# Hybrid decoder step on one core: first tile of x rounded by the Vector engine, queries taken out before a late weight chunk, keys turned before a subtraction, first softmax scaled by the Scalar engine

## The chip, the core and the metric

One core of a Trainium2 chip runs the whole program. The metric is the device time of one execution in microseconds, and a version is judged by the median of its runs. TensorE (PE) multiplies matrices, the Vector engine (DVE), the Scalar engine (ACT) and GpSimd (POOL) do elementwise work, and SyncE (SP) issues most of the loads.

## What is computed

The reference is one layer of a decoder for a prompt of 256 tokens and eight sample tokens, 264 columns in all, in fp32. Cut to what the change touches:

```
h = rmsnorm(x, g_mix)
proj = h @ w_in                       # pool channels | q | k | v, 512 columns each
q = rope(proj q); k = rope(proj k)    # 8 heads x 64
logits = q k^T * 64**-0.5, causal     # 256 x 256 per head for the prompt
p = softmax(logits);  attn = p v
x = x + concat(pool_out, attn) @ w_out
x = x + cross_attention(rmsnorm(x), memory)
x = x + relu(rmsnorm(x) @ w_up)**2 @ w_down
y = rmsnorm(x, g_final)
```

## The kernel before

**Products in three parts.** Every fp32 operand is split in a rounded part and a remainder ("hi" and "lo", both fp32r), and a product is hi\*hi + lo\*hi + hi\*lo. The weights stream through in 120 chunks of 256 rows by 512 columns. Per chunk SP loads `raw`, ACT copies it with rounding into `w_hi` (`split_hi`, line 1106 in the rows, since the helper `copy` records every ACT copy), and DVE subtracts into `w_lo` (`split_lo`, L1362). PE then runs 24 matmuls of 264 columns (four banks of 128 output rows, two row tiles, three passes, L1086). The splits run some chunks ahead: a chunk's `w_hi` goes into one of four buffers and waits until PE has used the chunk four before; its raw buffer is reloaded when an earlier chunk's `w_lo` is done.

**Start.** PE warms up with ten small fp32 matmuls (`warm_up`, L998). Then chunks 0 to 2 go row tile by row tile in `open_first_group` (L1010, L1013, L1016): hi weights on hi x, lo weights on hi x, hi weights on lo x, four matmuls each. ACT rounds the weights and x tile by tile; DVE makes both remainders. From chunk 3 on the ordinary loop runs.

**Groups and jobs.** Four chunks of `w_in` make one group: chunks 0 to 3 give the queries (banks 0 to 3), 4 to 7 the keys, 8 to 11 the values, 12 to 15 the pool channels `uext`. Each engine has its own program in one hand-written order. For every chunk it takes out the results of a finished group (`take_out`), does its share of the splits (`split_next`), and runs the jobs that the table in `plan_jobs` puts there. A ("split",) in that table says where among the jobs the split stands. Where a group ends and no such entry is there, `halfway` puts the split between the second and the third tile taken out.

**Jobs named later.** ("stat", "x"), after chunk 4, sums the squares of x on PE (L851, L855) in bank 0, which held the first query tile; ACT takes the root (L1258), DVE the reciprocal (L1556), and `turn_tables` multiplies the cosine and sine tables. ("turn", 0) turns the first pair of query tiles and ("turn", 2) the first pair of key tiles, four DVE instructions each (L1444 to L1448). ("S", 0) to ("S", 3), after chunk 8, are the scores of the first four heads (L829); PE waits in one place for both turns and for four free banks. ("exp", h) is on ACT; ("norm", 0), after chunk 13, inverts the row sums of four heads (L1534) and multiplies the four score tiles (L1539), both on DVE. ("P_T", h) transposes a head's probabilities on PE (L869), and ACT copies them out (`softT`). After chunk 15 come the scores of heads 4 to 7, in banks 3, 0, 1 and 4. Banks 3, 0 and 1 come free by the `softT` copies of heads 0 to 2, and bank 4 when DVE has taken out the first `uext` tile (L1403). ("v_nat", 0) and ("v_nat", 1), after chunks 12 and 13, are transposes of the values (L864) that ACT copies out and stores by a DMA of its own queue. ("m_tile", k) and ("m_lo", k) split the memory; each m_tile also makes a square that POOL adds (L1650).

Of the kernel before, what the change touches and what calls it, by code (L numbers as in the profile page):

```python
# [143 lines left out]


def plan_jobs():

# [17 lines left out]
    put(1, ("sum_x",), ("split",))  # L165
    put(2, ("split",))
    put(4, ("stat", "x"), ("tables",), ("split",), ("turn", 0))
    put(5, ("m_tile", 0))
    put(7, ("turn", 2), ("split",), ("m_tile", 1), ("m_tile", 2))
    put(8, ("m_tile", 3), ("m_lo", 0), ("m_lo", 1), ("m_lo", 2), ("S", 0), ("S", 1), ("S", 2), ("S", 3))  # L170
# [41 lines left out]

SCALED_BY_ACT = ()

# [205 lines left out]
def build(nc, ins, outs):  # L420
    with ExitStack() as ctx:
# [385 lines left out]
        def _(pe):  # L807
# [192 lines left out]
            def open_first_group():  # L1000

                for c in range(PARTED):
                    g, w, n, k, _ = CHUNKS[c]
                    hi, lo = hi_of(c), lo_of(c)
                    banks = banks_of(g)
                    for kk in range(CK):
                        pe.wait_ge(first_hi_ready, k + kk + 1)
                        pe.wait_ge(stream_hi, k + kk + 1)
                        for x, bank in enumerate(banks):
                            pe.matmul(psum[:, bank, 0:T], hi[:, kk, x * P:(x + 1) * P], act_hi[:, k + kk, :], start=k + kk == 0, stop=False)  # L1010
                        pe.wait_ge(first_lo_ready, k + kk + 1)
                        for x, bank in enumerate(banks):
                            pe.matmul(psum[:, bank, 0:T], lo[:, kk, x * P:(x + 1) * P], act_hi[:, k + kk, :], start=False, stop=False)  # L1013
                        pe.wait_ge(stream_lo, k + kk + 1)
                        for x, bank in enumerate(banks):
                            mm = pe.matmul(psum[:, bank, 0:T], hi[:, kk, x * P:(x + 1) * P], act_lo[:, k + kk, :], start=False, stop=False)  # L1016
                    mm.then_inc(w_used, 1)
# [86 lines left out]
        def _(act):  # L1104
# [35 lines left out]
            def take_out(c):  # L1140
# [3 lines left out]
                for x, bank in enumerate(banks_of(g)):  # L1144
                    src = psum[:, bank, 0:T]
                    k = AT * n + x
                    if x == 2 and halfway(c):
                        for s in SPLITS_AT.get(c + 1, ()):
                            split_hi(s)
# [159 lines left out]
            def split_next(c):  # L1309
                for s in SPLITS_AT.get(c + 1, ()):  # L1310
                    split_hi(s)

# [9 lines left out]
            for c in range(PARTED):  # L1322
                for kk in range(CK):
# [4 lines left out]
                    copy(hi_of(c)[:, kk, :], raw_of(c)[:, kk, :]).then_inc(first_hi_ready, 1)  # L1328
                    k = CK * c + kk
                    act.wait_ge(x_landed[k if k < 4 else CK * c], 16)  # L1330
                    copy(act_hi[:, k, :], xT[:, k, :], gains[:, GAIN["x"], k:k + 1]).then_inc(stream_hi, 1)
            round_x(3)
            for s in SPLITS_AT[0]:
                split_hi(s)
            for c in range(NC):
                if c == STAT_X:
                    act.wait_ge(tables_landed, 16)
                if CHUNKS[c][4]:
                    take_out(c)
                if not halfway(c) and ("split",) not in JOBS[c]:  # L1340
                    split_next(c)
# [8 lines left out]
        def _(dve):  # L1350
# [236 lines left out]
            def less_x(k):  # L1587
                dve.wait_ge(stream_hi, k + 1)
                less(act_lo[:, k, :], xT[:, k, :], gains[:, GAIN["x"], k:k + 1], act_hi[:, k, :]).then_inc(stream_lo, 1)

            dve.wait_ge(x_landed[0], 16)
            for c in range(PARTED):
                for kk in range(CK):
                    k = CK * c + kk
                    dve.wait_ge(first_hi_ready, k + 1)
                    V.tensor_tensor(lo_of(c)[:, kk, :], raw_of(c)[:, kk, :], hi_of(c)[:, kk, :].bitcast(F32), ALU.subtract).then_inc(first_lo_ready, 1)
                    less_x(k)
            for k in range(CK * PARTED, KT):
# [148 lines left out]
```

## Time and profile before

| | us |
|---|---|
| median of 3 runs (422.76, 421.59, 422.97) | 422.76 |
| the profiled execution's own time | 422.28 |
| its span in the profile | 420.1 |
| PE busy | 413.4 (98%) |
| DVE busy | 252.9 (60%) |
| ACT busy | 226.8 (54%) |
| granted TensorE clock, whole span | 0.999 |

The span is the stretch between the first and the last record. 2.18 us of the execution's own time lie outside it. A matmul's end is modelled: in a steady row a matmul is shown as 0.28 us long while the next begins 0.12 us after it, so a stall is best read from start to start, not from the idle time that is printed.

### The profile page before, as it was taken

How to read it: one execution, taken by the hardware profiler on the slowest of the kernel's cores; microseconds unless marked ns; L12 is line 12 of the kernel's file. 1: busy time of each engine (PE TensorE's matmuls, PEld its weight loads, DVE VectorE, ACT ScalarE, POOL GpSimd, SP SyncE). 2: the span in 40 equal slices, each digit the busy share in tenths (PEclk: the TensorE clock that was granted, in tenths of full speed). 3: DMA queues.
4: the chain of work that ended last, by engine and by line, in shares of the span. 5: the costliest groups of instructions: out<-in, count | busy, mean ns of one | idle time of the engine just before them, and what ended most of it. 6: DMA issues, size and time to landing. Idle time of an engine off the chain costs nothing.

```text
span 420.1 us, 8422 instructions
## 1 busy us (share of the span) xinstructions
PE 413.4 (98%) x3372; PEld 388.5 (92%) x3372; DVE 252.9 (60%) x398; ACT 226.8 (54%) x392; POOL 31.1 (7%) x41
## 2 busy tenths in 40 slices
PE   9999999999999999999999999999999999999995
PEld 8998989986879998958899999999999999999995
DVE  4899989666255785543269677766766534454302
ACT  6776958825364574423267566556565343453313
POOL 1003017000000120000022000000000000010010
PEclk9999999999999999999999999999999999999999
DMA  8999858974989966989527546545456555655002
GB/s 286 382 396 355 274 193 236 344 274 156 373 313 333 383 232 219 369 330 347 206 100 249 203 149 200 195 171 177 165 199 202 197 174 180 196 159 171 2 2 103
DMA packets 37257, 96.60 MB, mean 230 GB/s; under 512 B 4186, under 2 KB 13274, under 8 KB 37082
## 3 DMA queue, kind: packets, MB, share of 16 engines
q1 hardware_dynamic: 35250, 92.50, 63.2%
q10 hardware_dynamic: 1968, 3.55, 2.5%
q8 instruction: 27, 0.44, 0.4%
q14 instruction: 12, 0.10, 0.1%
HBM read 91.73 MB, written 4.54 MB: 229 GB/s over the span
## 4 chain that ended last, share of the span: by engine, by line
PE 90%; DMA 3%; DVE 3%; SPq 1%; issue 1%; ACT 0%; DVEq 0%
PE psum L1086 75%; PE psum L817 5%; PE psum L1031 2%; PE psum L945 2%; DMA raw<-in_w_in 2%; PE psum L932 2%; DMA pages<-in_page_table 1%; PE psum L829 1%; DVE w_lo L1362 1%; PE psum L869 1%; SPq L763 1%; PE psum L878 1%; PE psum L916 1%; PE psum L938 0%; DVE rstd L1556 0%
## 5 line engine op out<-in xcount | busy, mean ns | idle before, releaser
L1362 DVE TENSOR_TENSOR w_lo<-raw,w_hi 128x1024 fp32r<-128x1024 f32 x67 | 82.9, 1247 | 63.1 <-ACT w_hi L1106 62.9
L1106 ACT ACTIVATE w_hi<-raw 128x1024 fp32r<-128x1024 f32 (+1 forms) x73 | 73.9, 1020 | 60.1 <-PE psum L1086 48.0
L1086 PE MATMUL psum<-mix_hi,w_hi 128*128 128x264 f32 (+1 forms) x288 | 82.9, 288 | 0.0
L1086 PE MATMUL psum<-mix_lo,w_hi 128*128 128x264 f32 (+1 forms) x288 | 81.6, 283 | 0.0
L1086 PE MATMUL psum<-mix_hi,w_lo 128*128 128x264 f32 (+1 forms) x288 | 81.6, 283 | 0.0
L1086 PE MATMUL psum<-act_hi,w_hi 128*128 128x264 f32 x232 | 66.9, 288 | 0.0
L1086 PE MATMUL psum<-act_lo,w_hi 128*128 128x264 f32 x232 | 66.0, 284 | 0.0
L1086 PE MATMUL psum<-act_hi,w_lo 128*128 128x264 f32 x232 | 66.0, 284 | 0.0
L1086 PEld LDWEIGHTS psum<-mix_hi,w_hi 128*128 128x128 f32 x288 | 54.3, 189 | 0.9 <-issue 0.8
L1086 PEld LDWEIGHTS psum<-mix_lo,w_hi 128*128 128x128 f32 x288 | 54.2, 188 | 0.1
L1086 PEld LDWEIGHTS psum<-mix_hi,w_lo 128*128 128x128 f32 x288 | 54.1, 188 | 0.0
L1650 POOL TENSOR_TENSOR ssq<-ssq,sq 128x264 f32<-128x264 f32 (+1 forms) x27 | 22.5, 833 | 331.0 <-ACT sq L1127 329.6
L1086 PE MATMUL psum<-hid_hi,w_hi 128*128 128x264 f32 x160 | 45.5, 284 | 0.0
L1086 PE MATMUL psum<-hid_hi,w_lo 128*128 128x264 f32 x160 | 45.5, 284 | 0.0
L1086 PE MATMUL psum<-hid_lo,w_hi 128*128 128x264 f32 x160 | 45.4, 284 | 0.0
L1086 PEld LDWEIGHTS psum<-act_hi,w_hi 128*128 128x128 f32 x232 | 43.8, 189 | 0.4 <-issue 0.3
L1086 PEld LDWEIGHTS psum<-act_lo,w_hi 128*128 128x128 f32 x232 | 43.7, 188 | 0.0
L1086 PEld LDWEIGHTS psum<-act_hi,w_lo 128*128 128x128 f32 x232 | 43.6, 188 | 0.0
L1086 PEld LDWEIGHTS psum<-hid_lo,w_hi 128*128 128x128 f32 x160 | 30.1, 188 | 0.0
L1086 PEld LDWEIGHTS psum<-hid_hi,w_lo 128*128 128x128 f32 x160 | 30.1, 188 | 0.0
L1086 PEld LDWEIGHTS psum<-hid_hi,w_hi 128*128 128x128 f32 x160 | 30.1, 188 | 0.0
L1362 DVE TENSOR_TENSOR w_lo<-raw_more,w_hi 128x1024 fp32r<-128x1024 f32 x16 | 19.5, 1230 | 15.3 <-ACT w_hi L1106 15.3
(203 smaller groups left out, 811.1 us busy)
## 6 DMA issues: line engine op xcount, KB each, us to landing
raw<-in_w_down SPq DMA_DIRECT2D x20, 512.0 KB, 4.2
raw<-in_w_up SPq DMA_DIRECT2D x18, 512.0 KB, 3.7
raw_more<-in_w_up SPq DMA_DIRECT2D x14, 512.0 KB, 3.8
stage<-in_mem_v SPq DMA_DIRECT2D x12, 512.0 KB, 5.9
raw_more<-in_w_down SPq DMA_DIRECT2D x12, 512.0 KB, 4.4
stage<-in_cache_v SPq DMA_DIRECT2D x16, 256.0 KB, 6.5
keysT<-in_cache_k SPq DMA_DIRECT2D x16, 256.0 KB, 4.8
keysT<-in_mem_k SPq DMA_DIRECT2D x8, 512.0 KB, 6.4
```

The source lines that it names most:

```text
L763: sp.dma_start(raw_of(c)[:, kk, :], ins[w_of[w]][n, k // CK][:, kk, :]).then_inc(done, 16)
L817: return pe.matmul(out, lhsT, rhs, start=start, stop=stop, skip_group_check=True, tile_position=(0, 32 * j))
L829: last = pe.matmul(bank_of(job)[:, out:out + keys], qT[r:r + 32, f, queries:queries + P], kT[r:r + 32, f, 0:keys], start=half == 0, stop=h ...
L869: last = pe.transpose(B[:, x * P:(x + 1) * P], p[:, x * P:(x + 1) * P], ident)
L878: pe.matmul(o[:, 0:SEQ], v_nat[:, 0, h * HD:(h + 1) * HD], pT[:, 0:SEQ], start=True, stop=False, skip_group_check=True)
L932: last = pe.matmul(B[:, qt * MEM:(qt + 1) * MEM], q2T[:, 2 * h + d, qt * P:(qt + 1) * P], mkT[:, 2 * h + d, :], start=d == 0, stop=d == 1)
L945: last = pe.matmul(B[:, d * SEQ:(d + 1) * SEQ], mv[:, c, h * MHD + d * P:h * MHD + (d + 1) * P], pT[:, c * SEQ:(c + 1) * SEQ], start=c == ...
L1031: mm = pe.matmul(psum[:, bank, 0:T], a, b, start=False, stop=end_ and m == 2)
L1086: mm = pe.matmul(out, a, b, start=first and m == 0, stop=end_ and m == 2)
L1106: return nc.scalar.activation(out, in_, ACT.Copy, scale=scale)
L1362: V.tensor_tensor(lo_of(c), raw_of(c), hi_of(c).bitcast(F32), ALU.subtract).then_inc(w_lo_ready, 1)
L1650: nc.gpsimd.tensor_tensor(ssq[:, m % 2, 0:n], ssq[:, m % 2, 0:n], sq[:, k % SQ_SLOTS, 0:n], ALU.add).then_inc(sq_added, 1)
```

## The change

Four things are done.

1. DVE rounds the first tile of x (ACT skips it) and makes its remainder at once. PE's second pass on that tile is now hi weights on lo x, and lo weights come third. ACT waits for DVE's rounding before it rounds the second tile.
2. At chunk 3, where the queries are finished, ACT and DVE no longer split chunk 6 before it and chunk 7 halfway; all four query tiles are taken out first, and chunks 6 and 7 are split behind them.
3. ("turn", 2) moves from chunk 7 to chunk 6, ahead of the split of chunk 10.
4. `SCALED_BY_ACT` holds 0: the products of ("norm", 0) become eight ACT copies with a scale, two for each of the heads 0 to 3. DVE only inverts the sums. Heads 4 to 7 stay with DVE.

The core of the diff:

```
+QUERIES = last_chunk("in", 1)
...
     put(1, ("sum_x",), ("split",))
-    put(2, ("split",))
...
-    put(7, ("turn", 2), ("split",), ("m_tile", 1), ("m_tile", 2))
+    put(6, ("turn", 2), ("split",))
+    put(7, ("split",), ("m_tile", 1), ("m_tile", 2))
...
-SCALED_BY_ACT = ()
+SCALED_BY_ACT = (0,)
...
-                    if x == 2 and halfway(c):
+                    if x == 2 and halfway(c) and c != QUERIES:
...
             def split_next(c):
-                for s in SPLITS_AT.get(c + 1, ()):
-                    split_hi(s)
+
+                for at in {QUERIES - 1: (), QUERIES: (QUERIES, QUERIES + 1)}.get(c, (c + 1,)):
+                    for s in SPLITS_AT.get(at, ()):
+                        split_hi(s)
...
                     k = CK * c + kk
+                    if k == 0:
+                        continue
                     act.wait_ge(x_landed[k if k < 4 else CK * c], 16)
+                    if k == 1:
+                        act.wait_ge(stream_hi, 1)
...
             dve.wait_ge(x_landed[0], 16)
+            V.tensor_scalar(act_hi[:, 0, :], xT[:, 0, :], gains[:, GAIN["x"], 0:1], None, ALU.mult).then_inc(stream_hi, 1)
+            less_x(0)
```

The places on ACT and DVE, as the two programs have them (line number, operation, output from inputs, shape; a buffer is named by its tile). **ACT around the end of the queries (chunk 3), before:** the split of chunk 6 stands first, that of chunk 7 in the middle.

```order
L1209 ACTIVATE keysT<-x_and_gains 128x1056 x2
L1106 ACTIVATE w_hi<-more_keysT 128x1024
L1106 ACTIVATE w_hi<-raw 128x1024
L1106 ACTIVATE qT<-psum 128x264 x2
L1106 ACTIVATE w_hi<-raw 128x1024
L1106 ACTIVATE qT<-psum 128x264 x2
L1258 ACTIVATE std<-psum,const 128x266
```

After, in the same place:

```order
L1115 ACTIVATE qT<-psum 128x264 x4
L1115 ACTIVATE w_hi<-raw 128x1024 x2
L1267 ACTIVATE std<-psum,const 128x266
L1115 ACTIVATE w_hi<-raw 128x1024
L1115 ACTIVATE w_hi<-more_keysT 128x1024
```

The four copies of the queries moved ahead of both splits. The copies of chunk 5, as before, stand ahead of them.

**DVE from the query turn to the first scores, before:** the first four rows turn the queries, the second four the keys, with the subtractions of chunks 9 and 10 between them.

```order
L1444 SCALAR_TENSOR_TENSOR crossed<-qT,turned 128x264
L1445 SCALAR_TENSOR_TENSOR crossed<-qT,turned 128x264
L1446 SCALAR_TENSOR_TENSOR qT<-qT,turned 128x528
L1448 TENSOR_TENSOR qT<-qT,crossed 128x528
L1362 TENSOR_TENSOR w_lo<-more_keysT,w_hi 128x1024 x2
L1444 SCALAR_TENSOR_TENSOR crossed<-kT,turned 128x264
L1445 SCALAR_TENSOR_TENSOR crossed<-kT,turned 128x264
L1446 SCALAR_TENSOR_TENSOR kT<-kT,turned 128x528
L1448 TENSOR_TENSOR kT<-kT,crossed 128x528
L1362 TENSOR_TENSOR w_lo<-more_keysT,w_hi 128x1024
```

After:

```order
L1461 SCALAR_TENSOR_TENSOR qT<-qT,turned 128x528
L1463 TENSOR_TENSOR qT<-qT,crossed 128x528
L1377 TENSOR_TENSOR w_lo<-more_keysT,w_hi 128x1024
L1459 SCALAR_TENSOR_TENSOR crossed<-kT,turned 128x264
L1460 SCALAR_TENSOR_TENSOR crossed<-kT,turned 128x264
L1461 SCALAR_TENSOR_TENSOR kT<-kT,turned 128x528
L1463 TENSOR_TENSOR kT<-kT,crossed 128x528
L1377 TENSOR_TENSOR w_lo<-more_keysT,w_hi 128x1024 x2
```

One subtraction (chunk 10) moved from ahead of the keys' turn to behind it.

**ACT after chunk 13, before:** the second value tile, its store, the splits of chunks 17 and 18, a memory tile, and the copies of the transposed heads.

```order
L1106 ACTIVATE v_nat<-psum,rstd 128x512
L1268 DMA out_v_prompt<-v_nat 128x512
L1106 ACTIVATE w_hi<-raw 128x1024 x2
L1127 ACTIVATE sq<-stage 128x256
L1106 ACTIVATE mix_hi<-stage,x_and_gains 128x256
L1106 ACTIVATE softT<-psum 128x384 x3
```

After:

```order
L1277 DMA out_v_prompt<-v_nat 128x512
L1115 ACTIVATE soft<-soft,stats 128x128
L1115 ACTIVATE soft<-soft,stats 128x256
L1115 ACTIVATE soft<-soft,stats 128x128
L1115 ACTIVATE soft<-soft,stats 128x256
L1115 ACTIVATE soft<-soft,stats 128x128
L1115 ACTIVATE soft<-soft,stats 128x256
L1115 ACTIVATE soft<-soft,stats 128x128
L1115 ACTIVATE soft<-soft,stats 128x256
L1115 ACTIVATE w_hi<-raw 128x1024 x2
L1136 ACTIVATE sq<-stage 128x256
L1115 ACTIVATE mix_hi<-stage,x_and_gains 128x256
```

Eight scalings came in ahead of the splits of chunks 17 and 18 and of the copies of the transposed heads. On DVE the two products of L1539 are gone from behind the reciprocal (L1534), and the subtraction of chunk 17 follows it.

## Rows read from the trace of the kernel before

**Rows 1.** The page: span, then busy time, share and instructions of each engine.

```profile
span 420.1 us, 8422 instructions
PE 413.4 (98%) x3372; PEld 388.5 (92%) x3372; DVE 252.9 (60%) x398; ACT 226.8 (54%) x392; POOL 31.1 (7%) x41
```

**Rows 2.** Waits of PE over the span: who for whom, us in total, times, longest.

```profile
PE psum L829 <- DVE kT L1448: 0.6, 1, 0.6
PE psum L851 <- issue: 0.4, 1, 0.4
```

**Rows 3.** Timeline of the start (start us, length us, engine, line, operation).

```profile
5.21 0.42 PE L998 MATMUL psum<-std 128*128 128x128 f32 x1
5.50 0.97 PE L1010 MATMUL psum<-act_hi,w_hi 128*128 128x264 f32 x4
10.03 0.52 ACT L1106 ACTIVATE act_hi<-x_and_gains 128x264 fp32r<-128x264 f32 x1 [0.68 <-DMA x_and_gains<-in_x]
13.28 2.36 DVE L1362 TENSOR_TENSOR w_lo<-more_keysT,w_hi 128x1024 fp32r<-128x1024 f32 x2 [0.27 <-ACT w_hi L1106]
14.56 0.39 PE L1086 MATMUL psum<-act_hi,w_hi 128*128 128x264 f32 x1
```

**Rows 4.** Timeline of ACT and PE around the queries and the sum of x's squares.

```profile
19.65 1.06 ACT L1106 ACTIVATE w_hi<-raw 128x1024 fp32r<-128x1024 f32 x1 [2.40 <-DMA raw<-in_w_in]
20.61 0.65 ACT L1106 ACTIVATE qT<-psum 128x264 f32<-128x264 f32 x2
20.37 0.29 PE L1086 MATMUL psum<-act_hi,w_lo 128*128 128x264 f32 x1
21.08 0.68 PE L851 MATMUL psum<-ssq,const 128*128 128x264 f32 x2 [0.43 <-issue]
```

**Rows 5.** Landing times of the loads issued between 12.5 and 13 us (7.4 and 8.2).

```profile
DMA to landing us min/median/max: 7.4/7.8/8.2
```

**Rows 6.** Timeline of DVE and PE from chunk 7's subtraction to the first scores.

```profile
22.24 1.23 DVE L1362 TENSOR_TENSOR w_lo<-raw,w_hi 128x1024 fp32r<-128x1024 f32 x1 [0.28 <-ACT w_hi L1106]
28.73 0.71 DVE L1448 TENSOR_TENSOR qT<-qT,crossed 128x528 f32<-128x528 f32 x1
29.47 2.36 DVE L1362 TENSOR_TENSOR w_lo<-more_keysT,w_hi 128x1024 fp32r<-128x1024 f32 x2
31.75 0.43 DVE L1444 SCALAR_TENSOR_TENSOR crossed<-kT,turned 128x264 f32<-128x264 f32 x1
33.29 1.14 DVE L1448 TENSOR_TENSOR kT<-kT,crossed 128x528 f32<-128x528 f32 x1
33.60 0.29 PE L1086 MATMUL psum<-act_hi,w_lo 128*128 128x264 f32 x1
34.48 0.73 PE L829 MATMUL psum<-kT,qT 32*128 32x128 f32 x16 [0.60 <-DVE kT L1448]
```

**Rows 7.** Timeline of ACT from the first exponential to the transposed heads.

```profile
42.34 0.40 ACT L1230 ACTIVATE soft<-soft,stats 128x128 f32<-128x128 f32 x1
51.78 0.69 ACT L1106 ACTIVATE v_nat<-psum,rstd 128x512 f32<-128x512 f32 x1 [0.91 <-PE psum L864]
52.94 1.06 ACT L1106 ACTIVATE w_hi<-raw 128x1024 fp32r<-128x1024 f32 x1 [0.47 <-ACT v_nat L1106]
56.04 0.49 ACT L1106 ACTIVATE mix_hi<-stage,x_and_gains 128x256 fp32r<-128x256 f32 x1
56.44 1.23 ACT L1106 ACTIVATE softT<-psum 128x384 f32<-128x384 f32 x3
```

**Rows 8.** Timeline of POOL, DVE and PE before the second scores.

```profile
56.21 1.48 POOL L1650 TENSOR_TENSOR ssq<-ssq,sq 128x256 f32<-128x256 f32 x1 [14.77 <-ACT sq L1127]
57.00 0.97 DVE L1366 SCALAR_TENSOR_TENSOR mix_lo<-stage,x_and_gains,mix_hi 128x256 fp32r<-128x256 f32 x1
58.29 0.42 DVE L1403 TENSOR_TENSOR uext<-psum,rstd 128x264 f32<-128x264 f32 x1
58.86 0.39 PE L829 MATMUL psum<-kT,qT 32*128 32x128 f32 x4
```

More of the change, by code:

```diff
@@ L1010, in open_first_group @@
                             pe.matmul(psum[:, bank, 0:T], hi[:, kk, x * P:(x + 1) * P], act_hi[:, k + kk, :], start=k + kk == 0, stop=False)
+                        if k + kk == 0:
+                            pe.wait_ge(stream_lo, 1)
+                            for x, bank in enumerate(banks):
+                                pe.matmul(psum[:, bank, 0:T], hi[:, kk, x * P:(x + 1) * P], act_lo[:, 0, :], start=False, stop=False)
                         pe.wait_ge(first_lo_ready, k + kk + 1)
                         for x, bank in enumerate(banks):
[L1013 to L1016, printed above, removed]
+                            mm = pe.matmul(psum[:, bank, 0:T], lo[:, kk, x * P:(x + 1) * P], act_hi[:, k + kk, :], start=False, stop=False)
+                        if k + kk > 0:
+                            pe.wait_ge(stream_lo, k + kk + 1)
+                            for x, bank in enumerate(banks):
+                                mm = pe.matmul(psum[:, bank, 0:T], hi[:, kk, x * P:(x + 1) * P], act_lo[:, k + kk, :], start=False, stop=False)
                     mm.then_inc(w_used, 1)
@@ L1339, in _ @@
                     take_out(c)
-                if not halfway(c) and ("split",) not in JOBS[c]:
+                if (not halfway(c) or c == QUERIES) and ("split",) not in JOBS[c]:
                     split_next(c)
@@ L1596, in _ @@
                     V.tensor_tensor(lo_of(c)[:, kk, :], raw_of(c)[:, kk, :], hi_of(c)[:, kk, :].bitcast(F32), ALU.subtract).then_inc(first_lo_ready, 1)
-                    less_x(k)
+                    if k > 0:
+                        less_x(k)
             for k in range(CK * PARTED, KT):
```

## The prediction

> **What bounds the kernel now.** The page first: PE is busy for 413.4 us of the 420.1 [rows 1], so no other engine can set the time, and the time can only change by what PE waits. The list of PE's waits has, apart from the warm-up's start, two entries [rows 2]: 0.6 us at the first scores, which wait for the turned keys, and 0.4 us at the sum of x's squares, which is put down to no one. By the list PE never waits again behind the first scores. So the whole of what can be won lies in the first 35 us, and whatever is won there is PE's only if nothing that had been just in time becomes late. The timelines of the other engines are then read for that: who finishes how shortly before PE needs it.
>
> Matmul ends are modelled, so I take stalls from start to start. In a steady row a matmul starts 0.12 us after the last one. At the sum of squares the step is 21.08 - 20.37 = 0.71 us [rows 4], so PE loses 0.59 us. At the first scores it is 34.48 - 33.60 = 0.88 us [rows 6], so it loses 0.76 us. Together 1.35 us, 0.32% of the time.
>
> **First tile of x by DVE.** PE's first real matmul starts at 5.50, but the last warm-up pass only starts at 5.21 [rows 3], and PE works in order. The ten warm-up matmuls are twenty passes in the 4.4 us up to there, 0.21 us each, so PE isn't free before about 5.42: what an earlier first tile can bring is 0.08 us at once. A little more could come from the order of passes: the first four matmuls take 0.97 us. But it does not get far. Chunk 3 needs its `w_lo`, and that is the first of the two subtractions from 13.28, which ends at about 14.5 (2.36 us less one of 1.15 is 1.21); PE starts chunk 3 at 14.56 [rows 3]. It is just in time already. Its subtraction is set by ACT, which runs without a gap from 10.03 on, and at 10.03 ACT had waited 0.68 us for the fifth tile of x to land [rows 3]. Nothing of the change touches that load, which is issued before. So what PE wins at the start it waits at chunk 3. I count 0.0 us, bounds -0.1 and 0.0 (a loss is excluded as long as DVE has the tile by then, and its two extra-early instructions stand in time in which it was idle).
>
> **Queries first.** The sum of squares uses bank 0, and bank 0 is free when ACT has copied the first query tile. Before, that copy starts at 20.61, behind the rounding of chunk 6, which waited 2.40 us for its load and began at 19.65 [rows 4]. That is PE's 0.59 us. In the changed order ACT has nothing to do from 17.25 on (19.65 less the 2.40 it waited), takes the queries out as they come (chunk 3 ends at about 17.6) and is done by 18.5, in the time it waited. The load of chunk 6 decides its rounding as before, at 19.65. Chunk 7's rounding no longer has two query copies ahead of it, but its load was issued at 12.7 and took 8.2 us [rows 5], so it starts at 20.87 and not at 20.61, where 21.15 was (20.61 plus two copies). PE gets the sum of squares 0.59 us earlier: **-0.59 us**, and the rest is late by nothing: DVE's subtraction of chunk 7 goes from 22.24 [rows 6] to 21.96 and all that stands behind it on DVE comes 0.28 us earlier. The root on ACT now starts at about 21.85, the end of chunk 7's rounding, and is done before DVE wants it at 23.1.
>
> **Keys before the subtraction.** DVE works without a gap from 22.24 to the keys' turn. The turn starts at 31.75, and the two subtractions ahead of it take 2.28 us, 1.14 each [rows 6]. With one of them behind it and DVE 0.28 us ahead, the turn starts at 31.75 - 1.14 - 0.28 = 30.33. The two key tiles that it needs are there by then: chunk 8 ends at 33.72, chunks 7 and 8 are 24 matmuls of 0.122 us each, 2.93 us a chunk, so the first half of chunk 7 is done at 29.33, less 0.59, plus a copy of 0.4: 29.1. Its first three instructions take 33.29 - 31.75 = 1.54 us; the last took 1.14 us, 0.43 us more than the same one on the queries (0.71) [rows 6], which I take for POOL's doing (below). So the turn ends between 30.33 + 1.54 + 0.71 = 32.58 and 33.01. PE, 0.59 us ahead, gets to the scores at 33.60 - 0.59 + 0.12 = 33.13. Either end is in time, so the whole wait goes: **-0.76 us**. The subtraction of chunk 10, now behind the turn, ends by 34.6, and PE wants it at 37.6 (33.13, 1.53 for the scores and a chunk of 2.93). No DMA moves with it, and no load of weights waits for that one subtraction: its raw buffer isn't used again soon. From 33.13 on PE would be 1.35 us ahead of the kernel before.
>
> **Scaling on ACT.** DVE is rid of two products, which is no gain by itself, since it is not DVE's work that is late there before. ACT gets eight copies. The nearest rows for their price: a copy with a scale of 256 columns lasts 0.49 us and the next instruction starts 0.40 us after it (56.04 to 56.44) [rows 7]; an exponential of one of the very tiles, 128 columns, lasts 0.40 us [rows 7], so a step of 0.31. Four heads by 0.31 + 0.40 are 2.84 us. They stand ahead of the roundings of chunks 17 and 18 on ACT. PE needs those chunks only at 66 us, so this looks hidden. But DVE's order is: subtraction of 17, subtraction of 18, two remainders of the memory, and then the first `uext` tile, and PE's second set of scores waits for that tile's bank. Before, that tile starts at 58.29, is done at 58.71, and the scores start at 58.86 [rows 8]: 0.15 us apart, the tightest place of the stage.
>
> Follow it in the changed kernel. The chain begins with the second value tile on ACT, which waits for PE (51.78 [rows 7]), and PE is 1.35 us ahead: 50.43. ACT's own work up to there has room: the exponentials start at 42.34 [rows 7] behind a table load that came when PE's chunk 9 allowed it, and can start by about 41.2, when DVE has the maxima. From the value tile to the next work on ACT are 52.94 - 51.78 = 1.16 us (the copy and the DMA that it issues) [rows 7]: 51.59. The eight scalings: 54.43. Chunk 17's rounding takes a step of 0.96 us, so chunk 18's begins at 55.39 and is done at 56.45. DVE subtracts chunk 17 from 55.51 and chunk 18 from 56.66, 1.15 us each: 57.81. In the kernel before the remainders began at 57.00 and the `uext` tile at 58.29, 1.29 us later [rows 8]. So it starts at 59.10, is done at 59.52, and the scores start at about 59.57, where they were at 58.86. PE, which would have been 1.35 us ahead, waits about 2.06 us: **+2.06 us**. The copies of the transposed heads, also behind the scalings, end at 57.05 + 1.23 = 58.3 and are not last.
>
> The first remainder took 0.97 us (57.00), while POOL was adding a square, from 56.21 to 57.69 [rows 8]; two remainders undisturbed would be some 0.8 us. If POOL's addition falls elsewhere, 0.5 us of the 1.29 go, and the scores start at 59.07. I keep the 0.5, since the square comes at the same place of ACT's order, in chunk 18's subtraction, as before. The transposes of the heads 0 to 3 themselves are not late: the heads are ready at 52.3, 53.0, 53.7 and 54.4, and PE, 1.35 us ahead, wants them from 53.2 in steps of 0.33.
>
> A rule of the Trainium skill speaks against this edit: "ScalarE: Activation LUTs", Rules for kernel authors, gives multiplications to VectorE and not to ScalarE. By the section What ACT_TABLE_LOAD costs on the same page, a copy whose scale is a pointer takes 0.186 + 0.000833 per column in microseconds after overlap, estimated 2.77 us for the eight; the rows' 2.84 agree, and by the page's price the scores would start 0.07 us earlier. The rule compares the engines' speed; what decides here is the place in ACT's order.
>
> **The sum.** -0.59 - 0.76 + 2.06 = +0.71 us, by starts of the second scores 59.57 - 58.86. Behind them PE had no wait, and the stages are led by PE, so it stays: the execution of 422.28 us with its span of 420.1 becomes 423.0 with a span of 420.8. The median of the three runs, 422.76, is 0.48 us above that execution, and a run 1.2 us below it is among the three; I stay with the sum on the profiled time.
>
> **Rivals.** (a) The chain through the scalings is shorter: no POOL addition in the remainders (-0.5), and up to 0.6 us elsewhere, cheaper copies above all. The scores start at 58.5 to 58.9 and the net is -0.4 to 0.0: about 422.0. For it: POOL's addition only has to miss two short instructions. Against it: in the trace it was asked for during chunk 18's subtraction, too, and ran on over the remainder. (b) The scaling costs nothing: the scores don't wait for it, because the `uext` tile or the bank is free otherwise. Then the full 1.35 us are won: 420.9, faster by 0.32%. Against it stands the 0.15 us of slack and the order of DVE. (c) Slower: ACT's own chain ahead of the value tile does not come forward with PE. Its exponentials wait for the maxima, and DVE is only 0.28 us ahead. If the second value tile is copied at 51.5 and not at 50.43, everything behind is 1.07 us later: scores at 60.64, net +1.8, 424.1. It decides from a value tile later than 51.0 on (net over +1.27). For it: from 42.34 on ACT works nearly without a gap up to the value tile; against: its wait of 0.91 us there [rows 7], and exponentials that should begin 1.1 us earlier. (d) The change does not do what it says at the first two places: the load of chunk 7, at 8.2 us of landing, or the turn beside POOL comes later still, and PE is 0.9 us ahead, not 1.35. Since the second scores hang on PE's lead by way of the value tile, net is then about +1.2: 423.4.
>
> **Chances.** Forecast together with (d), -0.2 to +1.27 us: 0.53. (a), -0.2 to -1.27: 0.20. (b): 0.09. (c): 0.18. A measurement of this kernel can tell 0.3%, 1.27 us, from no change. So faster 0.09, same 0.73, slower 0.18. The likeliest time is 423.0. The range leaves out (b) below and the upper part of (c): 421.2 to 424.3.
>
> **What would show it.** In the profile of the changed kernel: PE's step to the sum of squares is 0.1 to 0.2 us and not 0.71; the scores start at about 33.1; chunk 3 starts at 14.5 to 14.6 although the first matmuls start a little earlier; eight ACT copies of 0.3 to 0.4 us stand from about 51.6 to 54.4; and PE has a new wait of 1.5 to 2.1 us at L829 near 57.6, for DVE's `uext`. If that wait is missing or under 1 us, the forecast is wrong and the time is below 422. If the second value tile's copy lies after 51.0, (c) is right. If the keys' turn ends after 33.2, (d).

## The result and the profile after

| | before | after |
|---|---|---|
| median, us | 422.88 (421.25 to 425.12, 20 runs) | 424.60 (422.62 to 425.69, 20 runs) |
| profiled execution's own time, us | 422.28 | 424.76 |
| its span, us | 420.1 | 422.6 |
| its granted clock | 0.999 | 0.996 |

The ratio is 1.0032, with an interval of 1.0019 to 1.0045: the changed kernel is slower by about 1.35 us (0.8 to 1.9). The two medians in the table stand further apart, 1.72 us; the ratio has an interval and is used from here on. The forecast was +0.71 us on the 422.28 of the profiled execution, with a range of 421.2 to 424.3. On that base the ratio gives 423.6 us, inside the range; the plain median of 424.60 lies 0.3 us above its upper end. The loss is about twice the forecast, and it lies just over the 0.3% that were taken as the border of "no change". The difference has to be looked for.

The page of the changed kernel, answering to [rows 1]:

```profile
span 422.6 us, 8428 instructions
PE 415.0 (98%) x3372; PEld 389.0 (92%) x3372; DVE 250.9 (59%) x397; ACT 229.5 (54%) x399; POOL 31.1 (7%) x41
```

PE has as many instructions as before and is "busy" 1.6 us longer. The list of its waits, answering to [rows 2] (who for whom, total, times, longest; the second is the warm-up's start):

```profile
PE psum L832 <- DVE uext L1418: 1.9, 1, 1.9
PE psum L1001 <- POOL std L1672: 1.0, 1, 1.0
```

Both waits of [rows 2] are gone, and one of 1.9 us has come. The timeline of PE, DVE and ACT from the start to the first scores, answering to [rows 3], [rows 4] and [rows 6]:

```profile
5.28 1.04 PE L1013 MATMUL psum<-act_hi,w_hi 128*128 128x264 f32 x4
14.69 0.39 PE L1095 MATMUL psum<-act_hi,w_hi 128*128 128x264 f32 x1
17.28 1.21 ACT L1115 ACTIVATE qT<-psum 128x264 f32<-128x264 f32 x4
19.62 1.06 ACT L1115 ACTIVATE w_hi<-raw 128x1024 fp32r<-128x1024 f32 x1 [1.13 <-DMA raw<-in_w_in]
20.50 0.28 PE L1095 MATMUL psum<-act_hi,w_lo 128*128 128x264 f32 x1
20.62 0.61 PE L854 MATMUL psum<-ssq,const 128*128 128x264 f32 x2
30.38 0.43 DVE L1459 SCALAR_TENSOR_TENSOR crossed<-kT,turned 128x264 f32<-128x264 f32 x1
31.93 0.71 DVE L1463 TENSOR_TENSOR kT<-kT,crossed 128x528 f32<-128x528 f32 x1
33.06 0.29 PE L1095 MATMUL psum<-act_hi,w_lo 128*128 128x264 f32 x1
33.27 0.94 PE L832 MATMUL psum<-kT,qT 32*128 32x128 f32 x20
```

The four query copies stand ahead of chunk 6's rounding, and PE's step to the sum of squares is 20.62 - 20.50 = 0.12 us. The keys' turn begins at 30.38, and the first scores follow the last matmul in 0.21 us: they begin at 33.27, where they began at 34.48. PE's lead is thus 1.21 us in this execution (chunk 3 had begun 0.13 us later than before, at 14.69).

The same for the stretch of the second scores, answering to [rows 7] and [rows 8]:

```profile
50.56 0.69 ACT L1115 ACTIVATE v_nat<-psum,rstd 128x512 f32<-128x512 f32 x1 [0.71 <-PE psum L867]
51.67 2.88 ACT L1115 ACTIVATE soft<-soft,stats 128x128 f32<-128x128 f32 x8 [0.42 <-ACT v_nat L1115]
54.45 1.99 ACT L1115 ACTIVATE w_hi<-raw 128x1024 fp32r<-128x1024 f32 x2
55.53 2.36 DVE L1377 TENSOR_TENSOR w_lo<-raw,w_hi 128x1024 fp32r<-128x1024 f32 x2 [4.48 <-ACT w_hi L1115]
57.81 1.34 DVE L1381 SCALAR_TENSOR_TENSOR mix_lo<-stage,x_and_gains,mix_hi 128x256 fp32r<-128x256 f32 x2
59.08 0.76 DVE L1418 TENSOR_TENSOR uext<-psum,rstd 128x264 f32<-128x264 f32 x2
57.29 0.49 PE L872 MATMUL psum<-const,soft 128*128 128x128 f32 x3
59.64 2.11 PE L832 MATMUL psum<-kT,qT 32*128 32x128 f32 x32 [1.86 <-DVE uext L1418]
61.68 3.06 PE L820 MATMUL psum<-keysT,qblock 128*32 128x257 f32 x32
64.68 0.65 PE L881 MATMUL psum<-softT,v_nat 128*64 128x256 f32 x4
```

DVE stands idle for 4.48 us until ACT, behind its eight scalings, has rounded chunk 17; then it works through its order, and PE gets the bank of the first `uext` tile at 59.64. That is 0.78 us after the 58.86 of [rows 8]. But the two groups of matmuls that follow are also longer. In the kernel before, the scores from 58.86 on were followed by (PE's timeline):

```profile
60.38 1.95 PE L817 MATMUL psum<-keysT,qblock 128*32 128x257 f32 x32
62.26 0.65 PE L878 MATMUL psum<-softT,v_nat 128*64 128x256 f32 x4
```

From the start of the scores to the start of the work behind both groups it was 62.26 - 58.86 = 3.40 us before and is 64.68 - 59.64 = 5.04 us after: 1.64 us more for the same 64 matmuls. The reason stands in the column of the granted clock (a row has the stretch and its length, then busy time and instructions of PE, PEld, DVE, ACT and POOL, then the clock, the share of DMA and GB/s):

```profile
core 0: us, PE busy (x) PEld busy (x) DVE busy (x) ACT busy (x) POOL busy (x), PEclk, DMA share, GB/s
58.00:59.00 1.00, 0.00 (x0) 0.00 (x0) 1.00 (x2) 1.00 (x2) 0.47 (x1) 1.00 0.87 283
60.00:61.00 1.00, 1.00 (x27) 1.00 (x24) 1.00 (x2) 0.00 (x0) 0.00 (x0) 0.79 0.04 16
61.00:62.00 1.00, 1.00 (x12) 0.23 (x11) 1.00 (x4) 0.00 (x0) 0.00 (x0) 0.50 0.06 16
63.00:64.00 1.00, 1.00 (x16) 0.54 (x12) 1.00 (x9) 1.00 (x4) 0.72 (x1) 0.51 0.34 47
64.00:65.00 1.00, 1.00 (x20) 0.40 (x14) 0.97 (x4) 0.56 (x3) 0.94 (x2) 1.00 0.00 0
```

PE does nothing in the whole microsecond from 58. About 0.9 us after it has begun again, at 60.6, its clock falls to 0.50, the lower of its two levels (1.2 of 2.4 GHz), and stays there until about 64. In the kernel before the column reads 1.00 in every one of these microseconds. So in this execution the loss of 2.5 us in span is 0.78 us of position and 1.64 us of clock (together 2.42). The clock of the whole span was 0.996 in the profile, and 0.995 or 0.996 in 8 of the 20 runs; those have a median of 424.77 us, the other twelve one of 423.97. The two slowest of the 20 (425.06 and 425.69 us) had a clock of 1.00, so the clock isn't the only thing that spreads the runs. In the experiments below the kernel before ran 89 times, and 5 of these runs were so low.

### The profile page after: what moved, and what is told of

Read it like the earlier page. It is cut to its first block, busy times and chain, and to the rows that moved or that the text cites. A ratio compares the mean times of both kernels' runs of the same rounds, so it can differ in the third digit from the quotient of the medians.

```text
span 422.6 us, 8428 instructions
## 1 busy us (share of the span) xinstructions
PE 415.0 (98%) x3372; PEld 389.0 (92%) x3372; DVE 250.9 (59%) x397; ACT 229.5 (54%) x399; POOL 31.1 (7%) x41
## 4 chain that ended last, share of the span: by engine, by line
PE 93%; ACT 2%; DVE 2%; DMA 1%; SPq 1%; issue 0%; DVEq 0%; ACTq 0%
PE psum L1095 77%; PE psum L820 5%; PE psum L1040 2%; PE psum L948 2%; PE psum L935 2%; DMA x_and_gains<-in_x 1%; PE psum L832 1%; DVE w_lo L1377 1%; ACT soft L1115 1%; SPq L766 1%; ACT w_hi L1115 1%; PE psum L881 1%; PE psum L919 1%; PE psum L941 0%; PE psum L854 0%; ACT act_hi L1115 0%
```

## The experiments

**Theory.** Everything but the clock is as the prediction had it: the first 35 us give PE up to 1.35 us, the scalings on ACT push `uext` back and cost some 2 us, and the wait of 1.9 us that comes of it is long enough to drop the clock in some of the executions, which costs once more. **Rivals.** The loss has nothing to do with the scalings (R1); the lower clock is chance and doesn't follow the wait (R2); the wait is set by the transposed heads and not by DVE (R3); the edits at the start give nothing, and what the profile shows of them is an accident of one execution (R4).

### The changed kernel with DVE's products

```
-SCALED_BY_ACT = (0,)
+SCALED_BY_ACT = ()
```

> The changed kernel with the first four heads scaled by DVE again; the other three edits stay. Theory: ACT's eight scalings ahead of the splits of chunks 17 and 18 are the whole of what the second scores wait for. Then the wait of 1.9 us at the second scores is gone, they start at 57.4 to 57.6 (58.86 before, 59.64 in the changed kernel), the granted clock stays at 1.00 between 57 and 66 us, and the time is the kernel before less 1.35 us, a ratio of 0.997 (0.995 to 0.999). Rival: the early lead of PE by itself makes the first uext tile late, with DVE's 1.8 us of scaling back ahead of the subtraction: a wait of 0.5 us or more stays and the ratio is 0.999 to 1.001.

Measured: 421.52 us (420.64 to 424.78, 12 runs), ratio to the kernel before 0.9968 [0.9949, 0.9986], a gain of 1.35 us. It equals the sum of PE's two stalls in [rows 4] and [rows 6] to the hundredth, which is luck: the interval is 0.8 us wide to either side. The second scores:

```profile
57.77 0.49 PE L872 MATMUL psum<-const,soft 128*128 128x128 f32 x3
58.20 1.59 PE L832 MATMUL psum<-kT,qT 32*128 32x128 f32 x32
```

No wait at all, though the scores start at 58.20 and not at the expected 57.4 to 57.6. In this execution the keys came late: PE waited 0.6 us for them at 33.83, since the weights of chunks 6 and 7 had landed late (ACT rounds them from 20.35 and 21.63 on, not from 19.62 and 20.91), so its lead is only 0.66 us at both scores. R1 falls: the whole loss is in the scalings, 1.0032 against 0.9968. So does the part of R4 that says that the start gives nothing.

### The kernel before with ACT's scalings alone

```
-SCALED_BY_ACT = ()
+SCALED_BY_ACT = (0,)
```

> The kernel before with ACT's scaling of the first four heads alone. Theory: the chain from the second value tile is as long as in the changed kernel and starts at 51.78, so the second scores start at 60.9 instead of 58.86, a wait of about 2.1 us, and the clock falls behind it as in the changed kernel, for another 1.7 us: a ratio of 1.005 (without the clock) to 1.009 (with it). Rival: the scaling hurts only because PE came early; with PE where it was, DVE's relief pays for most of it and the scores start before 59.6: 1.000 to 1.002.

Measured: 425.78 us (424.09 to 428.13, 6 runs), ratio 1.0075 [1.005, 1.010], +3.2 us.

```profile
PE psum L829 <- DVE uext L1403: 1.9, 1, 1.9
60.84 0.95 PE L829 MATMUL psum<-kT,qT 32*128 32x128 f32 x20 [1.86 <-DVE uext L1403]
```

Edit 4 alone moves the second scores from 58.86 to 60.84, +1.98 us, or 0.47%. The runs show 0.75%. The profiled execution is the fastest of the six (424.09 us, +1.81 to the 422.28 of before), and in it the clock stayed at 1.00 behind a wait of 1.86 us, as long as that of the changed kernel. Three of the six runs had a clock of 0.993 to 0.996 (425.25 to 428.13 us), but two with a clock of 1.00 took 425.77 and 426.32. So the wait alone does not decide in the single execution, and the clock does not account for all of the excess over 0.47%; the first of these speaks for R2, as far as it goes, and is taken up by the fillings below.

### The first tile alone, the queries alone, the keys alone

For the first tile, in the kernel before, edit 1 as it stands in the diff. For the queries:

```
+QUERIES = last_chunk("in", 1)
...
-    put(2, ("split",))
...
-                    if x == 2 and halfway(c):
+                    if x == 2 and halfway(c) and c != QUERIES:
...
-                for s in SPLITS_AT.get(c + 1, ()):
-                    split_hi(s)
+
+                for at in {QUERIES - 1: (), QUERIES: (QUERIES, QUERIES + 1)}.get(c, (c + 1,)):
+                    for s in SPLITS_AT.get(at, ()):
+                        split_hi(s)
...
-                if not halfway(c) and ("split",) not in JOBS[c]:
+                if (not halfway(c) or c == QUERIES) and ("split",) not in JOBS[c]:
```

For the keys:

```
-    put(7, ("turn", 2), ("split",), ("m_tile", 1), ("m_tile", 2))
+    put(6, ("turn", 2), ("split",))
+    put(7, ("split",), ("m_tile", 1), ("m_tile", 2))
```

> The kernel before with only the first tile of x rounded by DVE. Theory: PE's first real matmul starts at 5.3 and not at 5.50, and chunk 3 starts at 14.5 to 14.6 as before, because its subtraction is set by the landing of the fifth tile of x; the time is the same (0.999 to 1.001). Rival: the start sets the end, and chunk 3 begins 0.2 us earlier, with all behind it.

> The kernel before with the queries taken out ahead of chunks 6 and 7, and nothing else. Theory: PE's step to the sum of squares is 0.12 to 0.2 us and not 0.71; the first scores are still ended by the keys' turn, which comes 0.28 us earlier, at 34.2 for 34.48, so of the 0.59 us only 0.28 reach the second stage: ratio 0.999 to 1.000. Rival: the scores come 0.59 us earlier too.

> The kernel before with the keys' turn ahead of chunk 10's subtraction, and nothing else. Theory: the wait at the first scores goes, they start at 33.7 (0.76 us earlier), the sum of squares stays at 21.08, and all behind follows: second scores at 58.1, ratio 0.998 (-0.76 us). Rival: the turn meets POOL's additions or a late load and the scores start after 34.0.

Measured: the first tile 422.60 us (8 runs), 0.9997 [0.9978, 1.0017]; the queries 423.06 (10 runs), 1.0007 [0.9979, 1.0034]; the keys 422.17 (8 runs), 0.9976 [0.9942, 1.0010]. None of the three is told from no change by itself, and the keys alone are not told from the whole gain (0.9968) either.

The first tile, PE's timeline: the first matmul comes at 5.10, 0.40 us sooner than in [rows 3], and chunk 3 stands still, since PE waits for its remainder.

```profile
5.10 0.73 PE L1010 MATMUL psum<-act_hi,w_hi 128*128 128x264 f32 x4
14.71 0.39 PE L1092 MATMUL psum<-act_hi,w_hi 128*128 128x264 f32 x1 [0.59 <-DVE w_lo L1372]
```

The queries, in an execution in which the load of chunk 7 came late, the slowest of the ten runs (ACT's, DVE's and PE's timeline):

```profile
20.61 0.61 PE L853 MATMUL psum<-ssq,const 128*128 128x264 f32 x2
22.02 1.06 ACT L1108 ACTIVATE w_hi<-raw 128x1024 fp32r<-128x1024 f32 x1 [1.63 <-DMA raw<-in_w_in]
32.61 0.98 DVE L1448 SCALAR_TENSOR_TENSOR crossed<-kT,turned 128x264 f32<-128x264 f32 x1
35.24 1.17 DVE L1452 TENSOR_TENSOR kT<-kT,crossed 128x528 f32<-128x528 f32 x1
36.46 0.81 PE L831 MATMUL psum<-kT,qT 32*128 32x128 f32 x8 [3.13 <-DVE kT L1452]
```

The sum of squares comes in time (20.61), and 3.13 us are waited at the first scores: chunk 7 is rounded from 22.02 on, DVE's row up to the keys' turn begins that much later, and the turn itself is longer beside POOL. What the queries win at 20.6 is lost again here at the first scores. That edit 2 gives nothing without edit 3 is this one execution's reading; the ten runs leave room for the 0.28 us that were expected. This execution took 426.86 us and shows once more a low granted clock at a long wait. It fell at 35.8, while PE still stood, and was back at 42.6:

```profile
36.40:38.00 1.60, 1.54 (x24) 1.46 (x28) 1.57 (x3) 0.00 (x0) 0.00 (x0) 0.50 1.01 381
40.00:42.00 2.00, 2.00 (x11) 2.00 (x11) 2.00 (x15) 0.00 (x0) 0.00 (x0) 0.50 0.98 327
```

The keys, in an execution in which chunk 6 landed late, too:

```profile
20.48 1.06 ACT L1107 ACTIVATE w_hi<-raw 128x1024 fp32r<-128x1024 f32 x1 [3.18 <-DMA raw<-in_w_in]
21.92 0.68 PE L852 MATMUL psum<-ssq,const 128*128 128x264 f32 x2 [1.18 <-issue]
34.65 1.59 PE L830 MATMUL psum<-kT,qT 32*128 32x128 f32 x32
```

The first scores wait for nothing, but the sum of squares does, for 1.18 us: the first query tile still stands behind the rounding of chunk 6. They start at 34.65, not at the expected 33.7. In these two executions each edit removes one of two waits that a late load can cause, and the other wait takes up what was won. That is a reason to keep the two edits together, argued from one profile each; the medians don't prove it. R4 isn't refuted for any edit alone, but it is for the three together.

### `uext` sooner

Two memory remainders of DVE move behind the `uext` tile, in the changed kernel:

```
-    put(14, ("m_tile", 5), ("P_T", 0), ("m_lo", 3), ("m_lo", 4), ("P_T", 1), ("P_T", 2))
-    put(15, ("m_tile", 6), ("m_lo", 5), ("P_T", 3), ...
+    put(14, ("m_tile", 5), ("P_T", 0), ("P_T", 1), ("P_T", 2))
+    put(15, ("m_tile", 6), ("m_lo", 3), ("m_lo", 4), ("m_lo", 5), ("P_T", 3), ...
```

> The changed kernel with two remainders of the memory on DVE (tiles 3 and 4, 1.3 us) moved from ahead of the first uext tile to behind the four. Theory: the second scores wait for the later of uext (now at 57.8, done 58.2) and ACT's copies of the transposed heads (58.3): they start at 58.35 and not at 59.64, PE idles 0.8 and not 1.9 us, and with so short a wait the clock stays at 1.00. Ratio 0.998 to 0.999 (-0.5 us). If the clock falls all the same, +1.2 us: 1.002. Rival: uext is not what ends the wait; then they start at 59.6 as before.

Measured: 422.12 us (421.66 to 422.60, 12 runs), 0.9974 [0.9960, 0.9988]. DVE, ACT and PE:

```profile
58.05 0.77 DVE L1418 TENSOR_TENSOR uext<-psum,rstd 128x264 f32<-128x264 f32 x2
57.30 1.21 ACT L1115 ACTIVATE softT<-psum 128x384 f32<-128x384 f32 x3
58.77 1.59 PE L832 MATMUL psum<-kT,qT 32*128 32x128 f32 x32 [0.74 <-ACT softT L1115]
```

`uext` comes 1.03 us sooner, and the scores 0.87 us sooner: the last to release them now is ACT with the three `softT` copies. R3 is wrong for the changed kernel and right 0.87 us further on. The ratio came out below the expected 0.998 to 0.999. Against the changed kernel 0.58% are won, 2.4 us, where the position gives 0.87 us. Of the other 1.5 us the clock explains 0.66 on average (an estimate, worked out below); the remaining 0.9 us is about what the two intervals together leave open (0.8 us), and nothing in the profiles accounts for it. The profiled execution (422.60 us) is the slowest of the twelve. The clock was 1.00 in this stretch, and no run was below 0.997.

### The wait filled

Nine small matmuls of ones (18 passes) are put ahead of the second scores, in a bank that is free by then; the scores overwrite what they leave. They compute nothing that is used; they only keep PE at work while it waits. Once in the changed kernel, once in the kernel before with ACT's scalings:

```
+FILL = 9
...
                 pe.wait_ge(rope_done, turned_by(four, 2 + four))
+                if four == 1:
+                    begin(("S", 4))
+                    for _ in range(FILL):
+                        pe.matmul(bank_of(("S", 4))[:, 0:P], ones, ones, start=True, stop=True)
```

> The changed kernel with nine idle matmuls of 128 columns (about 1.9 us of PE, results overwritten) put in the wait ahead of the second scores, as soon as their first bank is free at 57.6. The scores can't start sooner than uext lets them. Theory: of the changed kernel's loss, the wait itself is 0.7 to 0.8 us and the rest, in the executions that have it, is the granted clock at 0.5 behind the wait. With PE busy the clock stays at 1.00 from 57 to 66 us in the profile, the second scores start at 59.6 to 59.8, and the ratio is 1.0015 to 1.002. Rival: the clock plays no part in the median, and the ratio stays at 1.0032 or rises.

> The kernel before with ACT's scaling alone and the same nine idle matmuls in the wait. Theory: the wait of 2.0 us stays (scores at 60.8 to 61.0) and what lay above it goes: a ratio of 1.0045 to 1.005, where the scaling alone gave 1.0075. Rival: no difference to the scaling alone, 1.0075.

Measured, filled against unfilled:

| | unfilled | filled | lowest clock of a run |
|---|---|---|---|
| the changed kernel | 1.0032 [1.0019, 1.0045] | 1.0012 [0.9992, 1.0033] | 0.995, filled 0.998 |
| before with ACT's scalings | 1.0075 [1.0050, 1.0100] | 1.0044 [1.0023, 1.0066] | 0.993, filled 0.997 |

DVE's `uext`, PE and its clock in the filled changed kernel:

```profile
59.82 0.76 DVE L1423 TENSOR_TENSOR uext<-psum,rstd 128x264 f32<-128x264 f32 x2
58.41 2.25 PE L829 MATMUL psum<-const 128*128 128x128 f32 x18
60.59 1.16 PE L837 MATMUL psum<-kT,qT 32*128 32x128 f32 x24
61.00:62.00 1.00, 1.00 (x28) 0.76 (x22) 1.00 (x3) 0.00 (x0) 0.00 (x0) 1.00 0.08 16
```

The filling doesn't bring the scores forward. They start at 60.59 here and not at 59.64: `uext` begins 0.74 us later, since PE waited 0.8 us for the keys at the first scores, and from `uext` to the scores it is 0.77 us where it was 0.56. The filling is thus itself about 0.2 us too long (in the second kernel, 60.67 filled and 60.84 unfilled, it is 0.76 and 0.56, too); a shorter one wasn't tried. And yet both kernels have lower ratios, by 0.20% and 0.31%, and not one of 24 runs has a clock of 0.996 or less, where 11 of the 26 unfilled ones have. In the second pair the filled kernel's loss agrees with the position alone: 60.67 - 58.86 = 1.81 us is 0.43%, measured 0.44% (0.23 to 0.66). R2 falls: the low clocks in excess of those of the kernel before (5 of 89) come of PE's standing still there. Each pair's intervals overlap, so the 0.2% and 0.3% are the best values and no more; that all low clocks are gone in both is the firmer part. The filled kernels ran on another chip than the one with ACT's scalings alone, but the kernel before had a low clock in 2 of 31 runs on the one and 2 of 35 on the other.

### The work shared

DVE multiplies heads 0 and 1, ACT heads 2 and 3 behind it:

```
-                    for h in range(4 * i[0], 4 * i[0] + 4):
+                    act.wait_ge(heads_ready, 2)
+                    for h in range(4 * i[0] + 2, 4 * i[0] + 4):
...
+                        dve.wait_ge(heads_inverted, four + 1)
+                        for x, (a, b) in enumerate(((0, P), (P, 3 * P))):
+                            last = V.tensor_tensor(soft[:, 0:2, a:b], soft[:, 0:2, a:b], stats[:, 0:2, 4 + x:5 + x].broadcast_to([P, 2, b - a]), ALU.mult)
+                        last.then_inc(heads_ready, 2)
```

> The changed kernel with heads 0 and 1 scaled by DVE and only heads 2 and 3 by ACT, behind DVE's. Theory: the chain to the uext tile is one half of the scaling shorter, 1.42 us, less up to 0.5 us that ACT waits for DVE: the second scores start at 58.2 to 58.8 instead of 59.64, PE waits 0.7 to 1.3 us for them, and the granted clock stays at 1.00. Ratio 0.998 to 0.9995, against 1.0032. Rival: the loss is not proportional to the scalings ahead of the splits, and the scores stay after 59.3.

Measured: 422.52 us (421.65 to 424.38, 12 runs), 0.9994 [0.9976, 1.0013].

```profile
51.93 1.49 ACT L1115 ACTIVATE soft<-soft,stats 128x128 f32<-128x128 f32 x4 [0.89 <-DVE soft L1554]
58.53 1.59 PE L832 MATMUL psum<-kT,qT 32*128 32x128 f32 x32 [1.04 <-DVE uext L1419]
```

With half of the scalings on ACT the scores come 1.11 us sooner than with all of them. It adds up: the scalings that are left take 2.88 - 1.49 = 1.39 us less, ACT waits 0.89 - 0.42 = 0.47 us more ahead of them, now for DVE, and the value tile came 0.20 us sooner (50.36), together 1.12. So each copy taken off ACT is worth its 0.35 us at the second scores, less what ACT then waits for DVE. The wait is 1.04 us, and the clock stays.

### The keys still sooner

The changed kernel with DVE's products, and on DVE the subtraction of chunk 9 goes behind the keys' turn as well:

```
-                if not halfway(c) and ("split",) not in JOBS[c]:
+                if not halfway(c) and ("split",) not in JOBS[c] and c != QUERIES + 2:
...
+                        if c == QUERIES + 3:
+                            split_next(c - 1)
```

> The changed kernel with the first four heads scaled by DVE again, and on DVE the keys' turn also ahead of chunk 9's subtraction, not only chunk 10's. Theory: what is left of the scatter and of the wait at the first scores comes from chunk 6's and 7's weights, which land between 19.3 and 22.0 us and start DVE's gapless row up to the turn. With 1.14 us less in that row, the first scores start at 33.1 to 33.3 with no wait even where those weights land 1 us late, and chunk 9's subtraction is done by 33.9, ahead of its use at 34.7. Ratio 0.995 to 0.997, not above the kernel with DVE's scaling alone (0.9968). Rival: the wait moves to chunk 9, and nothing is won.

Measured: 421.49 us (421.04 to 422.66, 12 runs), 0.9976 [0.9958, 0.9994].

```profile
31.04 0.71 DVE L1463 TENSOR_TENSOR kT<-kT,crossed 128x528 f32<-128x528 f32 x1
33.24 1.59 PE L832 MATMUL psum<-kT,qT 32*128 32x128 f32 x32
```

The turn is done at 31.75, 1.5 us ahead of the scores, which leaves room for a late load. The median is that of the kernel with the products on DVE (421.52), the slowest run is at 422.66 and not at 424.78. The ratio missed the expected 0.995 to 0.997 and isn't below that kernel's 0.9968. These two and the kernel with `uext` sooner (0.9974) are the best versions found, all three faster than the kernel before and the changed one; which is best, the runs don't tell.

## Why the prediction was right, and where it was short

**First tile: right.** 0.0 us forecast, 0.9997 measured alone, and chunk 3 at 14.69 and 14.71 where 14.5 to 14.6 were forecast. One step in its working was wrong and harmless: that PE isn't free before about 5.42. The first real matmul began at 5.28 and at 5.10. What it won was waited at chunk 3, as was said.

**Queries and keys: nearly right in the profile, and right as a sum (a gain of 1.35 us, 0.6 to 2.2, in the kernel that has only the first three edits). Too sure as single terms.** The sum of squares came in a step of 0.12 us, the turn at 30.38 (30.33 forecast), the scores at 33.27 (33.13), a lead of 1.21 us and not 1.35. But the working took the landing of two loads from one execution and held it fixed. ACT began to round chunk 6 anywhere from 18.93 to 20.52 us and chunk 7, where it waited for the load, from 20.65 to 22.02 in the profiles. The first scores of kernels with edits 2 and 3 waited 0.0 to 0.8 us, and those without edit 3 up to 3.1. Rival (d), a smaller lead, is thus not an alternative to the forecast but what happens in part of the executions.

**Scalings: right nearly to the step.** Second value tile at 50.56 (50.43), scalings from 51.67 to 54.45 (51.59 to 54.43), `uext` at 59.08 (59.10), scores at 59.64 (59.57). The position came out at +0.78, forecast +0.71. The last step of the forecast has a slip: before, the scores began 0.57 us behind the tile's start (58.29 to 58.86), so 59.10 leads to 59.67 and to +0.81, not to 59.57. A sign that the chain is the right one is that it holds with each part changed: with four of the eight scalings the 1.11 us that the scores come sooner are accounted for to 0.01, and with two short instructions of DVE less the next releaser is 0.87 us behind. Rival (a) fails: POOL added its square from 56.83 on and the two remainders and what lies about them took 59.08 - 57.81 = 1.27 us (1.29 forecast). Rival (b) fails by the wait of 1.86 us, rival (c) by the value tile, which came forward with PE.

**The rule about ScalarE.** The eight copies took 2.88 us here. The Trainium skill, "ScalarE: Activation LUTs", section What ACT_TABLE_LOAD costs, gave an estimated 2.77 for them: the trace agrees within 4%. Its Rules for kernel authors speak against the edit, and the edit lost, though not for the reason of speed: DVE did the two products in 1.83 us (in the kernel with the keys still sooner) and had the time, and what costs is that ACT's copies stand in order ahead of two roundings which DVE waits for.

**The step that failed: "Behind them PE had no wait, and the stages are led by PE, so it stays."** It treats the 1.9 us as a shift of everything behind it and leaves out what PE does after it has stood still. The term was put at zero. It is 1.64 us in the one profiled execution in which the clock fell there, and 8 of 20 runs show the mark of it, so an estimated 0.66 us on average. That estimate, 0.78 + 0.66 = 1.44 us, is to be held against the measured 1.35, and the forecast of 0.71 lacked the second part. The split of the 1.35 is not shown as firmly: the medians of the runs with and without the mark lie 0.80 us apart and not 1.64, which would make the second part 0.3 us. The filled waits are the evidence for it: with the scores no sooner and PE at work in the wait, the low clocks are gone, and 0.20% and 0.31% come back as best values.

What stays open: what decides in the single execution whether the clock falls. Behind waits of 1.86 us it fell in one profile and not in another; in the two kernels with waits of 0.74 and 1.04 us neither profile and none of the 24 runs showed it, nor did the profile of the first tile alone at a wait of 1.35 us ahead of the first scores, and at 3.13 us it fell. Only three profiles have a wait of over 1.8 us. Where in the other low runs the clock was low, their times can't tell. Nor is the difference between the twelve runs of the changed kernel at a clock of 0.997 and more (423.97, +1.1 us to the median of before) and the position (+0.78) explained; it is within what the runs can tell.

## What to carry to other kernels

Price an idle stretch of TensorE not by its length alone. A new wait of nearly 2 us in a stream of matmuls without a gap put everything behind it 0.78 us later and, where the clock fell, cost 1.64 us more; two of five runs have the mark of that. And before work is moved from one engine to another "with time to spare", follow what stands behind it in that engine's order to the first consumer on the critical engine: eight copies of a third of a microsecond ahead of two roundings, which PE did not need for some ten microseconds, cost 2 us by way of a subtraction that stood ahead of a tile whose bank was waited for. Where two waits can each be caused by a late load, removing only one may show nothing; measure both together before dropping either.

## What the runs showed of the hardware

**The granted clock can fall behind a wait of under 2 us.** PE stood still for 1.86 us before 59.64, and from 60.6 to 64 the clock was at 0.50. In the other case PE stood still for 3.13 us before 36.46, and the clock was at 0.50 from 35.8 to 42.6. The Trainium skill, "TensorE: Matmul & The Clock Gate", section What's actually happening, has an idle engine at 1.2 GHz and a busy one at 2.4: the level agrees with the 0.50 of the rows.

**A two-input instruction of DVE depends on what POOL does at its start.** The last instruction of the keys' turn took 0.71 us in the changed kernel and 1.17 where POOL had begun an addition 0.12 us before it:

```profile
35.12 0.72 POOL L1654 TENSOR_TENSOR ssq<-ssq,sq 128x256 f32<-128x256 f32 x1 [0.94 <-ACT sq L1129]
```

The Trainium skill, "SBUF — State Buffer", section Who interferes with whom, says that such a pair shares a port that the first one keeps for its whole instruction. The rows agree in which of the two is slowed: POOL was first here; in the changed kernel DVE was first (31.93), kept its 0.71 us, and it was POOL, from 32.18 on, that took 4.42 us for three additions (0.74 us for the one behind them). For how long the later one is held they don't agree so well: DVE lost 0.46 us, and POOL's addition had 0.60 us to run by its row.

**The same load of 512 KB, chunk 6, issued in the same place of each program, landed up to 1.6 us apart from one profiled execution to the other,** read from the start of the rounding that waited for it (18.93 to 20.52 us). In the six profiles of kernels with edits 2 and 3 the wait at the first scores follows it: none where the rounding began at 19.29, 19.37 and 19.62, then 0.2 us at 19.90, 0.6 at 20.35 and 0.8 at 20.52.
